# Feature sums of a block-wise feed-forward made tile by tile inside the output projections, one group fewer multiplied plainly, and one block addition moved ahead of the accumulator additions

## The chip, the cores and the metric

One core of a Trainium2 chip runs the whole program. The metric is the device time of one execution in microseconds, the median over runs of the same kernel. A change of 0.2% of it is about 6 us. TensorE multiplies matrices and writes to PSUM; VectorE and ScalarE work on SBUF and PSUM; POOL (GpSimd) works on SBUF; SP only issues transfers.

## The reference, cut to what matters

The model is two blocks over 1024 tokens of width 1024, all in float32. Each block ends with an output projection, a normalised residual, and a feed-forward network. The two networks have the same shape:

```
x = x + _rms_norm(mix, norm_post_mix[i])        # mix = [...] @ w_out
h = _rms_norm(x, norm_pre_ffn[i])
hid = h @ ffn_up                                # 1024 x 1024 times 1024 x 5632
hid = _causal_dwconv(hid, ffn_conv_w, ffn_conv_b)   # 3 taps along the tokens
gate, up = hid[..., :D_FF], hid[..., D_FF:]
f = (gelu(gate) * up) @ ffn_down                # 1024 x 2816 times 2816 x 1024
```

In the second block the activation is a SiLU and only the gate half has the three taps.

## The kernel before

Everything is float32 split into two parts: `hi` is the value rounded by ScalarE to the multiplier's format, `lo` is the rest, and a product is three matmuls: hi times hi, lo times hi, hi times lo.

`project_and_norm` is the output projection. It goes tile by tile over 128 tokens each: 48 matmuls (`product`), then for that tile a residual addition and a normalisation on VectorE with its statistics on ScalarE, then eight transposes on TensorE (`turn`), which put the normalised tile's features in PSUM (`turned`), and a `split` of them: ScalarE writes `hi`, VectorE `lo`. These are the features `blk_hi` and `blk_lo` of the feed-forward. The transposes of a tile stand two products behind its own product.

`feed_forward` handles the 2816 hidden columns in 22 groups of 128. For one group the up-projection has a gate half and an up half, so its weights are a 2 by 2 of blocks (half of the input features by gate and up), and the features are a 2 by 2 of blocks as well (half of the input features by half of the tokens). Groups 0 and 1 (`PLAIN = 2`) are multiplied plainly: two products of 48 matmuls of 512 columns, `plain_product`. All later groups use seven block products of 12 matmuls each in place of eight: P1, P6, P5, P2, P7, P3, P4. Their weight sums (S1 to S4) are made by POOL for each group; the feature sums T1 to T4 are made once. T1 = b12 - b11, T2 = b22 - T1, T4 = b21 - T2 and T3 = b22 - b12, where b11, b12 are the first half of the features for the first and second half of the tokens, and b21, b22 the second half. Before the change `t_sums(c)` makes them by VectorE for one 128-row chunk of features at a time, 10 additions of 128x512 each for four chunks; ScalarE rounds each sum and POOL (for the last chunk VectorE) subtracts.

One group is a `turn` on every engine. On TensorE it is the seven block products with 16 tiles of the down-projection (`down0` to `down15`, three matmuls each, for the group before) in four chunks between them: P1, P6, P5, P2, chunk, P7, chunk, P3, chunk, P4, chunk. VectorE adds each down tile to the accumulator in `x` (`add_down`) and combines the block products: u2 from P6, u3 and c22 from P7, c12 from P3, c21 from P4. The convolution's taps for the first half of the work follow (tapga, tapgb), the product gate times up is `hid`, and its rounding residue `hid_lo`. The first turn (`extra`) does the down-projections of both plain groups, the second one alone at its end. The last three turns ("alone" below) have no down tiles; there `M.skip(pe, j, 4)` stands in for each chunk, and makes TensorE's queue wait until its own last product is complete.

The order on each engine is the order in which the code is written; engines wait for each other on semaphores. `M`, `V`, `A` and `G` count what TensorE, VectorE, ScalarE and POOL have made in a turn. `following.first_dense` and `second_dense` are parts of group 0's first plain product, which are put between the last transposes of the output projection. ffn1 and ffn2, wout1 and wout2 are the names of the two networks and the two output projections.

## Time and profile before

| | us |
|---|---|
| median of 3 runs | 3067.23 (3066.8 to 3067.81) |
| the profiled execution, its own time | 3067.87 |
| its span in the trace | 3066.1 |
| TensorE busy in it | 2939.7 (96%) |
| mean granted TensorE clock | 0.983 |

How to read it: TensorE is the engine to look at. It is busy nearly all the time, and what it waits for in the few places where it does not work is what a change can win back. Busy time counts overlapped matmuls, so what a stretch costs is read from the starts of its rows.

### The profile page before, as it was taken

The numbers are of one execution on the slowest core, as the hardware profiler recorded it, in microseconds if no ns is written. First come the engines' busy times: TensorE is split into PE (matmuls) and PEld (weight loads), VectorE is DVE, ScalarE is ACT, GpSimd is POOL, SyncE is SP. The second block draws the span as 40 slices with busy tenths as digits, with TensorE's granted clock in tenths as the row PEclk, the third lists the DMA queues.
The fourth block names the chain that finished last, engine by engine and source line by source line (L and its number), as shares of the span: only waits on it lengthen the run. The fifth ranks groups of instructions, "written<-read, shape, count | busy, mean of one in ns | idle before, by whom it ended". The sixth has DMA issues, their size and how long they took to land. (4 is left out here: it accounts for less than half of the span.)

```text
span 3066.1 us, 55422 instructions
## 1 busy us (share of the span) xinstructions
PE 2939.7 (96%) x21756; PEld 2529.1 (82%) x21756; DVE 1974.5 (64%) x2682; ACT 1199.4 (39%) x1857; POOL 1198.7 (39%) x1035
## 2 busy tenths in 40 slices
PE   8999999996999999979999999999999799999998
PEld 6787888785788888768999999998978688888876
DVE  6898865567677777656465656663436666666644
ACT  3132544433233333343456555554323232323233
POOL 0003322325465656531343433432122455555562
PEclk9999999998999999999999999999999799999999
DMA  4111000311111112133111110112430111111112
GB/s 130 44 48 29 3 16 12 138 55 38 49 58 44 58 44 58 41 104 105 42 43 49 36 43 29 49 47 78 154 104 28 45 55 48 56 46 58 45 45 83
DMA packets 205489, 173.24 MB, mean 57 GB/s; under 512 B 10589, under 2 KB 182197, under 8 KB 204917
## 3 DMA queue, kind: packets, MB, share of 16 engines
q1 hardware_dynamic: 198389, 162.02, 17.2%
q10 hardware_dynamic: 6912, 8.52, 0.8%
q8 instruction: 142, 2.33, 0.3%
q14 instruction: 46, 0.38, 0.0%
HBM read 149.41 MB, written 21.10 MB: 56 GB/s over the span
## 5 line engine op out<-in xcount | busy, mean ns | idle before, releaser
L2930 DVE TENSOR_TENSOR tokens_x<-ffn_acc,tokens_x 128x512 f32<-128x512 f32 x450 | 296.4, 684 | 112.6 <-PE ffn_acc L2460 112.4
L3759 PE MATMUL mix_e<-blk_hi,mix_w_hi 128*128 128x348 f32 (+3 forms) x1056 | 346.8, 328 | 3.6 <-DVE blk_lo L2854 2.9
L3759 PE MATMUL mix_e<-blk_lo,mix_w_hi 128*128 128x348 f32 (+3 forms) x1056 | 339.8, 322 | 0.0
L3759 PE MATMUL mix_e<-blk_hi,mix_w_lo 128*128 128x348 f32 (+3 forms) x1056 | 338.9, 321 | 0.0
L2443 PE MATMUL ffn_out<-ffn_T,ffn_w12h 128*128 128x512 f32 x960 | 302.4, 396 | 21.5 <-DVE ffn_y L2898 7.5
L2460 PE MATMUL ffn_acc<-blk_hi,ffn_hid_hi 128*128 128x512 f32 x900 | 311.9, 396 | 9.3 <-DVE tokens_x L2930 5.7
L2443 PEld LDWEIGHTS ffn_out<-ffn_T,ffn_w12h 128*128 128x128 f32 x960 | 181.5, 191 | 62.8 <-POOL ffn_w12l L2362 15.6
L2362 POOL TENSOR_TENSOR ffn_w03l<-ffn_r,ffn_w03h 128x512 fp32r<-128x512 f32 x120 | 176.0, 1467 | 127.9 <-ACT ffn_w03h L2677 126.9
L2362 POOL TENSOR_TENSOR ffn_w12l<-ffn_r,ffn_w12h 128x512 fp32r<-128x512 f32 x120 | 174.3, 1462 | 122.5 <-ACT ffn_w12h L2677 110.2
L3285 POOL TENSOR_TENSOR mix_w_lo<-mix_raw,mix_w_hi 128x1024 fp32r<-128x1024 f32 x44 | 107.1, 2434 | 279.6 <-ACT mix_w_hi L3337 279.4
L2460 PEld LDWEIGHTS ffn_acc<-blk_hi,ffn_hid_hi 128*128 128x128 f32 x900 | 170.8, 190 | 46.7 <-issue 6.0
L3759 PEld LDWEIGHTS mix_e<-blk_hi,mix_w_hi 128*128 128x128 f32 x1056 | 199.1, 189 | 8.3 <-DVE blk_lo L2854 3.2
L3759 PEld LDWEIGHTS mix_e<-blk_lo,mix_w_hi 128*128 128x128 f32 x1056 | 199.0, 188 | 0.3
L3759 PEld LDWEIGHTS mix_e<-blk_hi,mix_w_lo 128*128 128x128 f32 x1056 | 198.9, 188 | 0.0
L2443 PE MATMUL ffn_out<-ffn_T,ffn_w12l 128*128 128x512 f32 x480 | 189.8, 396 | 0.0
L2460 PE MATMUL ffn_acc<-blk_hi,ffn_hid_lo 128*128 128x512 f32 x450 | 176.9, 393 | 0.0
L3300 POOL TENSOR_TENSOR mix_work<-mix_sf 128x128 f32<-128x128 f32 (+1 forms) x192 | 84.0, 437 | 209.9 <-DVE mix_sf L3600 181.5
L599 DVE SCALAR_TENSOR_TENSOR mixed_conv<-in_c,top_table,mixed_conv 128x1024 f32<-128x1024 f32 x120 | 155.9, 1299 | 3.8
L2677 ACT ACTIVATE ffn_w12h<-ffn_r 128x512 fp32r<-128x512 f32 x118 | 72.1, 625 | 213.2 <-PE ffn_out L2443 193.2
L2443 PE MATMUL ffn_out<-blk_hi,ffn_w03h 128*128 128x258 f32 (+1 forms) x480 | 130.1, 326 | 10.5 <-POOL ffn_w03l L2362 9.3
L2362 POOL TENSOR_TENSOR ffn_w12l<-ffn_S,ffn_w12h 128x512 fp32r<-128x512 f32 x40 | 53.6, 1341 | 208.3 <-ACT ffn_w12h L2677 194.2
L2677 ACT ACTIVATE ffn_w03h<-ffn_r 128x512 fp32r<-128x512 f32 x116 | 72.9, 630 | 155.1 <-PE ffn_out L2443 95.2
(494 smaller groups left out, 7493.3 us busy)
## 6 DMA issues: line engine op xcount, KB each, us to landing
ffn_r<-ffn_up SPq DMA_DIRECT2D x88, 256.0 KB, 3.0
mix_raw<-w_in SPq DMA_DIRECT2D x44, 512.0 KB, 3.9
ffn_r<-w_up SPq DMA_DIRECT2D x88, 256.0 KB, 3.0
ffn_room<-ffn_down SPq DMA_DIRECT2D x20, 512.0 KB, 4.0
ffn_room<-w_down SPq DMA_DIRECT2D x20, 512.0 KB, 3.9
proj_w_raw<-w_in_first SPq DMA_DIRECT2D x19, 512.0 KB, 3.8
branch_gates<-proj SPq DMA_DIRECT2D x16, 520.0 KB, 4.8
wout_raw<-w_out SPq DMA_DIRECT2D x16, 512.0 KB, 3.7
```

Of the source, the lines that this page charges most:

```text
L599: nc.vector.scalar_tensor_tensor(conv[:, f, :], c[:, f, t:t + T], table[:, column:column + 1], conv[:, f, :], ALU.mult, ALU.add).then_inc( ...
L2362: G.by(tt(slots[slot_][1], raw, slots[slot_][0], ALU.subtract), f"lo_{name}")
L2443: mm = nc.tensor.matmul(o, a[:, k, :], rhs, start=fresh and k == 0 and part == 0, stop=k == half - 1 and part == 2, skip_group_check=True)
L2460: mm = nc.tensor.matmul(accs[t % len(accs)], a[:, par, i * P:(i + 1) * P], b[:, h, :], start=part == 0, stop=part == 2)
L2677: A.by(activation(slots[slot_][0], raw, ACT.Copy), f"hi_{name}")
L2930: return vec.tensor_tensor(dst, accs[t % len(accs)], dst, ALU.add)
L3285: tt(w_lo[n % 2][:], raw[:], w_hi[n % 2][:], ALU.subtract).then_inc(lo_ready, 1)
L3300: tt(d4[:, :, 0, :], ref, a4[:, :, 0, :], ALU.subtract)
L3759: last = nc.tensor.matmul(dst[:, 0:m], a[n % 2][:, kd, :], b[:, kd, c:c + m], start=kd == 0 and part_ == 0, stop=kd == KD - 1 and part_ == 2)
```

## The change

The diff does seven things.

1. The feature sums are made by tiles of 128 tokens (all four feature chunks at once, still 128x512 elements an operation), `token_sums`, from the transposed tile in PSUM rather than from hi and lo in SBUF: T1a = b12(PSUM) - h11, T1 = T1a - l11, T2 = b22(PSUM) - T1, T3a = b22(PSUM) - h12, T3 = T3a - l12, T4a = h21 - T2, T4 = T4a + l21. That is 7 operations for each of 4 tile pairs, 28 in place of 40. Tile 4 pairs with tile 0, 5 with 1, 6 with 2, 7 with 3.
2. The output projections take the tiles in the order 0, 1, 4, 2, 5, 3, 6, 7 (the second one with the 16 meta rows third), and the sums of tiles 4 and 5 stand inside the projection's loop, those of 6 and 7 behind it. The transposes of a tile move from two products behind to inside the next product, before its last chunk.
3. ScalarE rounds T2, T1, T3 of tiles 4 and 5 at the end of the projection (`early_hi`), POOL subtracts them there (`early_lo`); the remaining lo parts of tiles 6 and 7 (8 operations) are VectorE's (`DVE_LO`), T4 of tiles 4 and 5 POOL's.
4. The raw sums lie in places that are free then, some of them those of the weights of group 0's second product. Therefore `second_load` waits for POOL's first two early subtractions, and ScalarE rounds those weights after six.
5. Only group 0 is plain. The first turn does group 1, with the down-projection of group 0; there is no extra down-projection. TensorE waits for each T before the first product that needs it (`wait_block`), and for `plain_tap` (the taps of the plain group) before P1 and P6.
6. In every turn, VectorE's s5 = P5 + x stands ahead of `down0` to `down3`, and c22 = P7 + s5 follows P7; u3 is gone. P3, which adds to P5's bank, waits for s5 rather than for c22, and P4 for c22 rather than u3.
7. In the alone turns TensorE's queue waits for its own completion only once, behind P4 (and not in the last).

```
-    tile_at = [0, 1, NT] + list(range(2, NT)) if meta_src is not None else list(range(NT))
+    tile_at = [0, 1, NT, 4, 2, 5, 3, 6, 7] if meta_src is not None else [0, 1, 4, 2, 5, 3, 6, 7]
...
             for i in range(2, tiles):
                 if mixed or i > 2:
                     pe.wait_ge(psum_free, i - (1 if mixed else 2))
-                for k in order:
+                for n, k in enumerate(order):
+                    if i == 2 and n == KD - 1:
+                        turn(0)
+                    if i == 3 and n == 3:
+                        turn(1)
+                    if i >= 3 and n == KD - 1:
+                        turn(i - 1)
                     mm = product(i, k)
                 mm.then_inc(product_ready, 1)
-                turn(i - 2)
-            turn(tiles - 2)
...
+                before = tile_at[i - 1] if 0 < i < tiles - 1 else None
+                if before in (4, 5):
+                    following.token_sums(dve, before, turned_of(i - 1), ("T1a", "T3a"))
+                if i == tiles - 1:
+                    following.token_sums(dve, 5, turned_of(i), ("T4a", "T4"))
...
+                if before == 4:
+                    following.token_sums(dve, 4, turned_of(i - 1), ("T1", "T2", "T3", "T4a", "T4"))
+                if before == 5:
+                    following.token_sums(dve, 5, turned_of(i - 1), ("T1", "T2", "T3"))
...
+            for name in names:
+                dst, a, b, op, after = ways[name]
+                if after:
+                    dve.wait_ge(t_step, summed(t, after))
+                vec.tensor_tensor(dst, a, b, op).then_inc(t_step, 1)
...
                 def downs(chunk):
                     if not has_down:
-                        M.skip(pe, j, 4)
+                        if chunk == 3 and not last:
+                            M.skip(pe, j, 2 * NT)
                         return
...
                 G.wait(pe, j, "lo_P3")
-                V.wait(pe, j, "c22")
+                V.wait(pe, j, "s5")
                 M.by(block_product(1, b22, [bank_c], False), "P3")
                 downs(2)
                 G.wait(pe, j, "lo_P4")
-                V.wait(pe, j, "u3")
+                V.wait(pe, j, "c22")
...
                 downs(3)
-                if extra:
-                    pe.wait_ge(extra_lo, 1)
-                    pe.wait_ge(plain_hid_lo, 2)
-                    V.wait(pe, j, DOWN[-1])
-                    for t in range(2 * NT):
-                        if t >= len(accs):
-                            pe.wait_ge(extra_added, t - len(accs) + 1)
-                        down_tile(1, t).then_inc(extra_down, 1)
...
+                M.wait(dve, j, "P5")
+                if second and first:
+                    dve.wait_ge(plain_hid_lo, 1)
+                    dve.wait_ge(plain_hid_hi, 1)
+                elif second:
+                    V.wait(dve, j, "hid_lo")
+                V.by(vec.tensor_tensor(uu[:, 512:T], bank_c, xbuf, ALU.add), "s5")
                 downs(0, 1, 2, 3)
                 M.wait(dve, j, "P7")
...
             V.skip(dve, 0, len(dve_names))
-            t_sums(0)
+            for t, name in DVE_LO[0:4]:
+                t_split_lo(dve, vec.tensor_tensor, t, name, t_dve_lo)
             plain_taps(0)
-            t_sums(1)
+            for t, name in DVE_LO[4:]:
+                t_split_lo(dve, vec.tensor_tensor, t, name, t_dve_lo)
             plain_taps(1)
             plain_hidden(0)
             plain_hidden_lo(0)
-            t_sums(2)
-            plain_taps(2)
-            t_sums(3)
```

How VectorE's order moves between the first output projection and the first network. Before, from the last normalisation (L2098) and the last two splits to the plain group's taps (L2898):

```order
L2098 SCALAR_TENSOR_TENSOR wout1_normed_7158<-tokens_x_49,wout1_inv_7161,wout1_gains_7164 128x1024
L2066 TENSOR_TENSOR blk1_lo_51<-wout1_out2,blk1_hi_50 128x8x128
L2066 TENSOR_TENSOR blk1_lo_51<-wout1_turned0,blk1_hi_50 128x8x128
...
L2861 TENSOR_TENSOR ffn1_t_raw0_7150<-blk1_hi_50 128x512
L2861 TENSOR_TENSOR ffn1_t_raw0_7150<-ffn1_t_raw0_7150,blk1_lo_51 128x512 x2
...
L2861 TENSOR_TENSOR ffn1_t_raw3_7153<-ffn1_t_raw3_7153,blk1_lo_51 128x512 x2
L2898 SCALAR_TENSOR_TENSOR ffn1_y_7142<-ffn1_out0,top_table,ffn1_y_7142 128x1023
```

Now, from the last residual addition (L2110) over the last normalisation (L2122) to the same taps (L2956); `ffn1_acc` is the transposed tile in PSUM:

```order
L2110 TENSOR_TENSOR tokens_x_49<-wout1_scaled_7173,tokens_x_49 128x1024
L2459 TENSOR_TENSOR ffn1_t_place1_7151<-blk1_hi_50,ffn1_t_low4_7162 128x512
L2459 TENSOR_TENSOR ffn1_t_place1_7151<-ffn1_t_place1_7151,blk1_lo_51 128x512
...
L2122 SCALAR_TENSOR_TENSOR wout1_normed_7168<-tokens_x_49,wout1_inv_7171,wout1_gains_7174 128x1024
L2459 TENSOR_TENSOR ffn1_t_place2_7152<-ffn1_acc,blk1_hi_50 128x512
...
L2083 TENSOR_TENSOR blk1_lo_51<-ffn1_acc,blk1_hi_50 128x8x128
...
L2428 TENSOR_TENSOR ffn1_T2_7137<-ffn1_y_7142,ffn1_T2_7137 128x4x128
...
L2956 SCALAR_TENSOR_TENSOR ffn1_y_7142<-ffn1_out0,top_table,ffn1_y_7142 128x1023
```

Between the last normalisation and the taps of group 0 there stand now the split of tile 7, 14 sums of tiles 6 and 7 and four lo parts; before it was two splits and ten sums, with thirty more sums behind the taps. Two sums (T4a and T4 of tile 5) stand ahead of the last normalisation.

VectorE in a turn, from u2 to c22. Before:

```order
L2961 TENSOR_TENSOR ffn1_ug_7143<-ffn1_out1,ffn1_room_7149 128x512
L2930 TENSOR_TENSOR tokens_x_49<-ffn1_acc,tokens_x_49 128x512 x4
L2976 TENSOR_TENSOR ffn1_uu_7144<-ffn1_out1,ffn1_room_7149 128x512
L2978 TENSOR_TENSOR ffn1_uu_7144<-ffn1_out0,ffn1_uu_7144 128x512
L2930 TENSOR_TENSOR tokens_x_49<-ffn1_out1,tokens_x_49 128x512
```

Now:

```order
L3019 TENSOR_TENSOR ffn1_ug_7143<-ffn1_out1,ffn1_room_7149 128x512
L3033 TENSOR_TENSOR ffn1_uu_7144<-ffn1_out0,ffn1_room_7149 128x512
L2988 TENSOR_TENSOR tokens_x_49<-ffn1_acc,tokens_x_49 128x512 x4
L3037 TENSOR_TENSOR ffn1_uu_7144<-ffn1_out1,ffn1_uu_7144 128x512
L2988 TENSOR_TENSOR tokens_x_49<-ffn1_out1,tokens_x_49 128x512
```

The first addition into `uu` now reads P5's bank (`out0`) and stands ahead of the four accumulator additions; one addition, not two, follows P7.

TensorE at the end of the first output projection, before: the last product, the transposes of tiles 5 and 6, then group 0's first matmuls.

```order
L1968 MATMUL wout1_out1<-wout1_w_lo3_77,blk1_hi_50 128x512 x2
L1984 MATMUL wout1_turned0<-top_ident,wout1_normed_7158 128x128 x8
L1984 MATMUL wout1_out2<-top_ident,wout1_normed_7158 128x128 x8
L2425 MATMUL ffn1_out0<-blk1_hi_50,ffn1_w03h_7130 128x512
```

Now:

```order
L1971 MATMUL wout1_out1<-wout1_w_lo2_76,blk1_hi_50 128x512 x2
L1990 MATMUL ffn1_acc<-top_ident,wout1_normed_7168 128x128 x8
...
L1971 MATMUL wout1_out1<-wout1_w_lo3_77,blk1_hi_50 128x512 x2
L2530 MATMUL ffn1_out0<-blk1_hi_50,ffn1_w03h_7130 128x512
```

The transposes of tile 6 stand ahead of the last six matmuls of the last product, and none stand between it and group 0. In both kernels tile 7's transposes follow 24 matmuls later.

## Rows read from the trace of the kernel before

**Rows 1.** Busy time by stretch: start:end, length, each engine's busy us, PEclk granted, DMA.

```profile
641.00:652.95 11.95, 11.95 (x57) 9.86 (x56) 5.26 (x6) 3.77 (x7) 0.96 (x1) 1.00 0.11 44
680.60:701.40 20.80, 12.83 (x49) 10.01 (x49) 17.37 (x15) 5.62 (x7) 7.60 (x5) 0.83 0.09 25
811.73:842.00 30.27, 30.27 (x134) 24.81 (x133) 22.67 (x28) 10.66 (x15) 18.20 (x13) 1.00 0.18 53
...
2456.60:2487.10 30.50, 30.50 (x158) 25.98 (x156) 17.54 (x25) 9.78 (x14) 16.64 (x12) 1.00 0.17 52
```

**Rows 2.** Timeline of TensorE, start of ffn1: start, us, line, [idle before <- who ended it].

```profile
652.95 1.03 PE L1984 MATMUL wout_turned<-top_ident,wout_normed 128*128 128x128 f32 x8
680.59 0.80 PE L2425 MATMUL ffn_out<-blk_hi,ffn_w03h 128*128 128x512 f32 x1 [2.44 <-POOL ffn_w03l L2347]
701.39 1.22 PE L2425 MATMUL ffn_out<-blk_hi,ffn_w12h 128*128 128x512 f32 x2 [7.97 <-POOL ffn_w12l L2347]
720.05 0.80 PE L2443 MATMUL ffn_out<-blk_hi,ffn_w03h 128*128 128x512 f32 x1 [4.62 <-POOL ffn_w03l L2362]
732.75 1.19 PE L2443 MATMUL ffn_out<-ffn_T,ffn_w12h 128*128 128x512 f32 x2 [7.54 <-DVE ffn_y L2898]
768.72 0.77 PE L2460 MATMUL ffn_acc<-blk_hi,ffn_hid_hi 128*128 128x512 f32 x1 [5.65 <-DVE tokens_x L2930]
781.47 0.40 PE L2443 MATMUL ffn_out<-blk_hi,ffn_w03h 128*128 128x512 f32 x1
```

**Rows 3.** The same for the start of ffn2.

```profile
2336.39 1.91 PE L1984 MATMUL wout_turned<-top_ident,wout_normed 128*128 128x128 f32 x16
2377.70 1.22 PE L2425 MATMUL ffn_out<-blk_hi,ffn_w12h 128*128 128x512 f32 x2 [4.64 <-POOL ffn_w12l L2347]
2396.36 0.80 PE L2443 MATMUL ffn_out<-blk_hi,ffn_w03h 128*128 128x258 f32 x2 [4.64 <-POOL ffn_w03l L2362]
2408.86 1.19 PE L2443 MATMUL ffn_out<-ffn_T,ffn_w12h 128*128 128x512 f32 x2 [7.50 <-DVEq L2918]
2442.91 0.80 PE L2460 MATMUL ffn_acc<-blk_hi,ffn_hid_hi 128*128 128x512 f32 x1 [3.62 <-POOL blk_hi L2395]
2456.58 0.40 PE L2443 MATMUL ffn_out<-blk_hi,ffn_w03h 128*128 128x258 f32 x2
```

**Rows 4.** VectorE's feature sums in 663 to 742 by form, then timeline rows of VectorE and POOL.

```profile
L2861 DVE TENSOR_TENSOR ffn_t_raw<-ffn_t_raw,blk_lo 128x512 f32<-128x512 f32 x24 | 28.3, 1179 | 0.8
...
668.78 0.69 DVE L2861 TENSOR_TENSOR ffn_t_raw<-ffn_t_raw,blk_lo 128x512 f32<-128x512 f32 x1
669.51 1.67 DVE L2861 TENSOR_TENSOR ffn_t_raw<-blk_hi,ffn_t_raw 128x512 f32<-128x512 f32 x1
676.22 2.60 DVE L2898 SCALAR_TENSOR_TENSOR ffn_y<-ffn_out,top_table,ffn_y 128x1023 f32<-128x1023 f32 x2
...
669.14 3.18 POOL L2355 TENSOR_TENSOR ffn_T<-ffn_t_raw,ffn_T 128x512 fp32r<-128x512 f32 x2 [3.12 <-ACT ffn_T L2635]
676.92 1.30 POOL L2355 TENSOR_TENSOR ffn_T<-ffn_t_raw,ffn_T 128x512 fp32r<-128x512 f32 x1 [2.02 <-ACT ffn_T L2635]
```

**Rows 5.** Timeline of VectorE: the normalisation of the last tile, wout1 and wout2.

```profile
659.11 1.28 DVE L2098 SCALAR_TENSOR_TENSOR wout_normed<-tokens_x,wout_inv,wout_gains 128x1024 f32<-128x1024 f32 x1
...
2340.08 1.28 DVE L2098 SCALAR_TENSOR_TENSOR wout_normed<-tokens_x,wout_inv,wout_gains 128x1024 f32<-128x1024 f32 x1
```

**Rows 6.** Timeline of TensorE in the first alone turns of ffn1, and c21 on VectorE.

```profile
1265.63 0.40 PE L2443 MATMUL ffn_out<-blk_hi,ffn_w03h 128*128 128x512 f32 x1
1277.16 0.70 PE L2443 MATMUL ffn_out<-ffn_T,ffn_w03h 128*128 128x512 f32 x2 [0.30 <-PEq L118]
1281.78 0.47 PE L2443 MATMUL ffn_out<-blk_hi,ffn_w12h 128*128 128x512 f32 x1 [1.60 <-DVEq L118]
1292.22 0.70 PE L2443 MATMUL ffn_out<-ffn_T,ffn_w12h 128*128 128x512 f32 x2 [0.84 <-DVEq L118]
...
1291.39 0.69 DVE L2990 TENSOR_TENSOR ffn_uu<-ffn_out,ffn_room 128x512 f32<-128x512 f32 x1
```

More of the change, by code:

```diff
@@ L2267, in sync, with turn @@
         def sync(sp):
-            def turn(g, par, has_down, extra=False, last=False):
+            def turn(g, par, has_down, first=False, last=False):
                 j = turn_of(g)
-                if extra:
-                    sp.wait_ge(t_step, 10 * half)
-                    sp.wait_ge(plain_up, 2 * PLAIN)
+                if first:
+                    sp.wait_ge(plain_up, 2)
                     load_down(sp, 0)
@@ L2376, in next_group, with turn @@
                 G.by(tt(R12, R12, R11, ALU.subtract), "S4")
-            def turn(g, par, has_down, extra=False, last=False):
+            def turn(g, par, has_down, first=False, last=False):
                 j = turn_of(g)
@@ L2462, in down_tile, with turn @@
                 return mm
-            def turn(g, par, has_down, extra=False, last=False):
+            def turn(g, par, has_down, first=False, last=False):
                 j = turn_of(g)
@@ L2490, in turn @@
                 V.wait(pe, j, "c21", back=1)
-                if extra:
-                    pe.wait_ge(t_lo_ready, 4 * half)
-                    pe.wait_ge(plain_tap, 2 * PLAIN)
+                if first:
+                    wait_block(pe, "T2")
+                    pe.wait_ge(plain_tap, 2)
                 M.by(block_product(1, block_t(T2_), [bank_b], True), "P6")
@@ L2671, in last_split, with turn @@
                     last_hi_ready, 1)
-            def turn(g, par, has_down, extra=False, last=False):
+            def turn(g, par, has_down, first=False, last=False):
                 j = turn_of(g)
@@ L2930, in add_down, with turn @@
                 return vec.tensor_tensor(dst, accs[t % len(accs)], dst, ALU.add)
-            def turn(g, par, has_down, extra=False, last=False):
+            def turn(g, par, has_down, first=False, last=False):
                 j = turn_of(g)
```

309 lines of the change are left out of this document (165 added, 144 removed), and 3 rows, old and new, of the table SUM_STEPS.

## Prediction

> **What bounds the kernel now.** I read the windows first. In a turn of either network TensorE is busy for all of its 30.27 us (ffn1, 132 matmuls: 0.229 each) or 30.50 us (ffn2), at the full clock, 2.4 GHz, while VectorE has 22.67 and less [rows 1]. The loop's turns are at TensorE's own pace, so whatever is only hidden work there is worth nothing. A projection tile is the same: TensorE busy 11.95 of 11.95 us, VectorE 5.26 [rows 1]. TensorE's timeline then shows where it does wait, and that is in one place per network: between the end of the output projection and the first turn of the loop. In ffn1 the last projection product ends at 652.95 and the turn of group 3 starts at 781.47: 128.5 us, with five waits of 2.44, 7.97, 4.62, 7.54 and 5.65, together 28.2 us [rows 2]. In ffn2 it is 2336.39 to 2456.58, 120.2 us, with 4.64, 4.64, 7.50 and 3.62, 20.4 us [rows 3]. The waits cost more than themselves: after the first, 48 matmuls take from 680.59 until 7.97 before 701.39, so 12.8 us, where 48 times 0.229 is 11.0 [rows 2]; the granted clock of this stretch is 0.83, a part of it at 1.2 GHz after an engine that stood still [rows 1].
>
> How much of it is loss: three sets of transposes 2.4 us (1.91 for two of them, [rows 3]), four plain products at 11.0 (44.0; group 0's first, in pieces, about 0.3 more), a turn 30.3 and 48 down matmuls 11.0, sum 88.0. So 40 us of ffn1's 128.5 are waits and slow clock. For ffn2 the same count, a little more for its gate products of 72 shorter matmuls, gives 89.5 of 120.2, so 31 us.
>
> The waits name POOL's weight residues and `plain_tap`, and both are late for the same reason. VectorE is busy 17.37 of 20.80 us in such a stretch [rows 1], with sums; they are also slower than they need be. A sum takes 0.69 us, but 1.67 when POOL subtracts at the same time; the 24 of one form have a mean of 1.179 [rows 4]. The tap operations, two in 2.60, are not slowed though POOL runs inside them at 676.92: they read one operand from PSUM, the sums two from SBUF [rows 4]. By the Trainium skill (SBUF — State Buffer, Who interferes with whom) a VectorE instruction with two SBUF inputs and a POOL instruction that reads SBUF exclude each other for a whole instruction, one with at most one SBUF input does not; the trace agrees, with 0.98 us more for a sum and nothing for a tap. I count 0.95 for each such meeting.
>
> **The parts.** Times are from P, the end of the last projection product. In the new kernel two transposes that followed it come before it, so P itself is 1.6 us later (two times 0.8); it is added at the end.
>
> *Sums of tiles 4 and 5 in the projection.* 14 operations of 0.72 (0.69 and a gap) in tiles where VectorE idles 6.7 of 11.95 us [rows 1]: hidden, except that the transposes of the tile after tile 4 overwrite its PSUM and wait for its T2. That is ready at about P+7.4 of that tile plus two to three operations, 9 to 10 us; the transposes come at 7/8 of the next product, 9.6. I take 0.5 us per projection, 1 together; if all of it is exposed, 2.
>
> *The last tile.* Before, its normalisation ends at 660.39, 7.4 us after P [rows 2, 5], just what two sets of transposes and 24 matmuls (1.9 + 5.5) cover. Now only 5.5 cover it, so TensorE waits 1.9 in any case. T4a and T4 of tile 5 and POOL's six early subtractions (1.30 each, [rows 4]) now fall there as well; three two-SBUF operations that meet POOL give 3 us more. So the transposes at P+10.5 in ffn1. In ffn2, which has no first normalisation, it ended at 2341.36, P+5.0 [rows 3, 5]; ScalarE's rounding of the tile before no longer stands in this chain (half a microsecond), two meetings give 1.9: P+6.4. The slow clock after such a wait costs 1.8, as at 680.59 (12.8 for 11.0); I count 1.9.
>
> *VectorE from there to P6.* In ffn1: 14 sums and 8 lo parts of 0.72 (15.8), the split 1.2, two pairs of taps 5.2: 22.2. Sixteen of these operations read two SBUF operands. POOL has less to do than before, but its group sums S1 to S4 and weight residues fall here: I take six meetings (5.7), between none and 16 (15.2). P6 waits for the second taps: 10.5 + 22.2 + 5.7 = 38.4. TensorE's own work until P6 is 10.5 + 0.8 + 5.8 + 11.0 + 2.7 + 1.9 = 32.7, so it waits 5.7 around P1. In ffn2 one pair of taps (2.6) and a multiplication (1.4): 6.4 + 15.8 + 1.2 + 2.6 + 1.4 + 5.7 = 33.1.
>
> *The rest, to the loop's same point* (the start of the turn of group 3). After P6's start 30.3 less P1's 2.8, the turn of group 2, and the slow clock: 48 matmuls took 720.05 - 4.62 - 701.39 = 14.0 after the wait of 7.97 and 781.47 - 768.72 = 12.8 after that of 5.65, where 11.0 is the full clock's, so 3.0 and 1.8 [rows 2]; I take 2.3 and 2.0. ffn1: 38.4 + 27.5 + 30.3 + 2.3 + 1.6 = 100.1, against 128.5: **28.4 won**. ffn2: 33.1 + 27.6 + 30.5 + 2.0 + 1.6 = 94.8 against 120.2: **25.4 won**. Of each, 2.7 us are matmuls that no longer exist (12 of 0.229); the rest is waits and clock. The weights of group 0's second product, now loaded later, need six POOL subtractions (until P+11 to 13), a rounding and a POOL subtraction of twice the size (2 x 1.30, [rows 4]): ready about P+16, while the first product ends at 10.5 + 0.8 + 5.8 + 1.9 = P+19. Hidden by 3 us in ffn1, some 1 to 2 in ffn2; without that cover they would cost what they exceed it by.
>
> *s5 ahead of the down additions.* In the loop P3 begins one chunk of 12 matmuls (2.7 us) after P7 ends, and u3 and c22 take 1.4: hidden already, worth nothing. VectorE waits for `down0` there, so s5 costs nothing either. In the alone turns no chunk covers it: P7 to P3 takes 1281.78 - 1277.16 = 4.6, of which 2.7 are matmuls and 1.6 the wait [rows 6]. But P6 of the next turn starts when c21 is done (1291.39 + 0.69 = 1292.08, P6 at 1292.22, [rows 6]), and c21 stands behind taps whose inputs come from POOL's and ScalarE's chain that starts at P7's end. So in the first two alone turns the gap moves from P3 to P6, and only the last turn keeps 1.6 to 2. The queue's wait ahead of P7 (1265.63 to 1277.16 is 11.5 for 48 matmuls, 11.0) is won three times: 0.5 each. Together 3.5 per network, 7 for both; if no chain takes P3's place 3 x 2.5 x 2 = 15, if the end of the network is also bound elsewhere, 2.
>
> **The sum.** 28.4 + 25.4 + 7 - 1 = 59.8; from the profiled execution's own time, 3067.9, that is 3008.1. The median of the runs shown is 0.6 lower, so **3007.5**.
>
> Bounds of the likeliest case: one to two meetings more or less in each network and the alone turns at 2 or 15 give about 2996 to 3018.
>
> **The rivals.** *VectorE is not the bound* (15%). For it: the sums from PSUM do not meet POOL, and there are only 14 left. Then TensorE's own work sets P6, 27.7 at P+7.4 without a slow clock, VectorE's 29.6; P6 at 29.6 and no clock loss is 8.8 + 2.3 better in ffn1, and in ffn2 the same count gives 27.4 in place of 33.1 and 2 of clock, 7.7: 3007.5 - 18.8, about 2989. Against it: VectorE was the busiest engine here.
>
> *Every two-SBUF operation meets POOL* (17%): ten more meetings a network, 9.5 each, 19: 3026. The Trainium skill's page SBUF — State Buffer (SBUF: two separate sides) says that whichever of the two starts first keeps the port for its whole instruction; the 0.98 us above agree. For it: a mean of 1.179 against 0.69 is half of those sums met already [rows 4]. Against: the eight lo parts start before P1's weights are free for POOL.
>
> *The early sums stretch the projections* (5%): if every tile from the fourth on waited 1 to 2 us for its transposes, ten tiles, 3018 to 3028. The windows' 6.7 idle us of VectorE speak against it.
>
> *Slower* (4%): s5 must be done before P3, and stands ahead of four accumulator additions, on which `down5` to `down8` wait. If in the loop VectorE came to it late, all 32 looped turns would stretch; it decides from 59.8 / 32 = 1.9 us a turn on. With 2.5 us each, 80 in all, it would be 3088. Against it: VectorE idles 7.6 us of a turn [rows 1], and P5 ends one whole product before the chunk whose additions it precedes.
>
> *The change does little* (2%): if the waits at the start stay where they are because the last taps alone set them, only the removed matmuls and the alone turns count, 12 us: 3055; and no change within 0.2% at all would need these to be lost too.
>
> **How the numbers follow.** Likeliest case 57%. Range 2990 to 3026: from the first rival to the second; outside it remain half of the first rival, a part of the second, and the last three. A measurement tells 6 us, 0.2%, from no change. Faster 0.95, same 0.01, slower 0.04.
>
> **What would show it.** Right: the span from P to the turn of group 3 near 100 and 95 us, TensorE's waits there three (before tile 7's transposes, before P1, before P6), VectorE without idle from P to the taps, a loop turn of 30.3 and 30.5 as before, a P7 to P3 of 2.7 in the alone turns with a longer wait before P6. Wrong: TensorE waiting inside the projections, a POOL weight residue as the last releaser, or a turn in the loop longer than 30.5.

## The result, and the profile after

The changed kernel takes 3022.88 us (median of 4 runs, 3017.51 to 3025.36); the kernel before, timed beside it, takes 3067.02. The ratio is 0.985 (0.9838 to 0.9862), 44 us less. Timed once more beside other kernels it took 3018.50 (5 runs, 3013.22 to 3019.09) against 3066.84: 0.9838 (0.9822 to 0.9853), 48 us less. The prediction was 3007.5, with 59.8 us won.

P is again the end of the last projection product. The windows of the changed kernel (start:end, length, busy time of PE, PEld, DVE, ACT, POOL, granted clock, DMA), for the stretches of [rows 1]: a projection tile, the stretch from tile 7's transposes to P6, a looped turn of ffn1 and one of ffn2:

```profile
649.60:661.55 11.95, 11.95 (x57) 9.83 (x56) 5.34 (x7) 3.88 (x7) 0.95 (x1) 1.00 0.11 44
671.80:701.60 29.80, 24.20 (x116) 20.84 (x117) 29.31 (x29) 14.13 (x20) 21.02 (x14) 0.84 0.09 26
790.86:821.13 30.27, 30.27 (x134) 24.80 (x132) 23.15 (x29) 10.95 (x15) 18.46 (x13) 1.00 0.19 53
2442.62:2473.12 30.50, 30.50 (x157) 26.00 (x156) 20.62 (x26) 9.79 (x14) 17.39 (x13) 1.00 0.17 53
```

Tile and turns last as long as before. VectorE is busy 29.31 of 29.80 us before P6, so it is what TensorE waits for there. TensorE's timeline at the start of ffn1, to set beside [rows 2] (P; tile 7's transposes; P1 and P6 of the first turn; the turns of groups 2 and 3):

```profile
661.55 0.40 PE L2530 MATMUL ffn_out<-blk_hi,ffn_w03h 128*128 128x512 f32 x1
671.82 1.97 PE L1990 MATMUL ffn_acc<-top_ident,wout_normed 128*128 128x128 f32 x8 [4.50 <-DVE wout_normed L2122]
696.37 0.77 PE L2548 MATMUL ffn_out<-blk_hi,ffn_w03h 128*128 128x512 f32 x1 [5.58 <-DVE ffn_y L2956]
701.63 0.76 PE L2548 MATMUL ffn_out<-ffn_T,ffn_w12h 128*128 128x512 f32 x2
729.28 0.40 PE L2548 MATMUL ffn_out<-blk_hi,ffn_w03h 128*128 128x512 f32 x1
...
760.59 0.40 PE L2548 MATMUL ffn_out<-blk_hi,ffn_w03h 128*128 128x512 f32 x1
```

Five long waits have become two, and P to the turn of group 3 is 99.04 us, where it was 128.5. The same view of ffn2, to set beside [rows 3]; here it is 95.15 us for 120.2:

```profile
2316.96 0.32 PE L2530 MATMUL ffn_out<-blk_hi,ffn_w03h 128*128 128x344 f32 x1
2323.77 1.97 PE L1990 MATMUL wout_turned<-top_ident,wout_normed 128*128 128x128 f32 x8 [2.81 <-DVE wout_normed L2122]
2348.55 0.77 PE L2548 MATMUL ffn_out<-blk_hi,ffn_w03h 128*128 128x258 f32 x2 [3.72 <-DVE ffn_y L2953]
...
2412.11 0.40 PE L2548 MATMUL ffn_out<-blk_hi,ffn_w03h 128*128 128x258 f32 x2
```

Timeline rows of VectorE, then of POOL, in the same stretch of ffn1, for [rows 4, 5]: the first sum ahead of the last normalisation, that normalisation, a lo part, the second taps; and POOL's early subtractions:

```profile
666.10 1.78 DVE L2459 TENSOR_TENSOR ffn_t_place<-blk_hi,ffn_t_low 128x512 f32<-128x512 f32 x1
669.67 2.10 DVE L2122 SCALAR_TENSOR_TENSOR wout_normed<-tokens_x,wout_inv,wout_gains 128x1024 f32<-128x1024 f32 x1
690.28 1.76 DVE L2428 TENSOR_TENSOR ffn_T<-ffn_y,ffn_T 128x512 fp32r<-128x512 f32 x1
698.54 2.59 DVE L2956 SCALAR_TENSOR_TENSOR ffn_y<-ffn_out,top_table,ffn_y 128x1023 f32<-128x1023 f32 x2
...
663.79 3.54 POOL L2428 TENSOR_TENSOR ffn_T<-ffn_t_low,ffn_T 128x512 fp32r<-128x512 f32 x2 [5.69 <-ACT ffn_T L2424]
668.97 5.15 POOL L2428 TENSOR_TENSOR ffn_T<-ffn_t_low,ffn_T 128x512 fp32r<-128x512 f32 x3
```

Operations of VectorE with two SBUF operands take 1.76 and 1.78 here where a sum alone took 0.69 [rows 4], and the normalisation 2.10 for 1.28 [rows 5]; the taps are not slowed. POOL's subtractions take 1.7 each in place of 1.30: a meeting (such an operation of VectorE at the same time as one of POOL) costs both engines. TensorE and, in the last row, c21 on VectorE in the first turns of ffn1 without down tiles, for [rows 6]:

```profile
1264.55 0.47 PE L2548 MATMUL ffn_out<-blk_hi,ffn_w03h 128*128 128x512 f32 x1 [0.30 <-PEq L118]
1271.37 0.70 PE L2548 MATMUL ffn_out<-ffn_T,ffn_w12h 128*128 128x512 f32 x2 [3.79 <-DVEq L118]
1291.17 0.51 PE L2548 MATMUL ffn_out<-blk_hi,ffn_w03h 128*128 128x512 f32 x1 [1.45 <-POOL ffn_w03l L2470]
1298.59 0.69 PE L2548 MATMUL ffn_out<-ffn_T,ffn_w12h 128*128 128x512 f32 x2 [4.37 <-DVEq L118]
...
1270.53 0.69 DVE L3049 TENSOR_TENSOR ffn_uu<-ffn_out,ffn_room 128x512 f32<-128x512 f32 x1
```

No row waits at P3 any more; P6 waits 3.79 and 4.37, until c21 is done (1271.22). Cutting the three profiled executions (before; after; after once more, the run e7 below) at the same points gives, with turn 19 the first one without down tiles, and the "last transposes" those of the first full tile of tokens at the end of ffn1:

| stretch | before | after | after, e7 |
|---|---|---|---|
| start of the program to P | 652.95 | 661.55 | 654.68 |
| P to the turn of group 3, ffn1 | 128.52 | 99.04 | 95.89 |
| the loop, to turn 19 | 484.16 | 484.18 | 484.20 |
| turn 19 to the last transposes of ffn1 | 105.99 | 106.61 | 105.89 |
| from there over the second mixer to P | 964.77 | 965.58 | 965.32 |
| P to the turn of group 3, ffn2 | 120.19 | 95.15 | 95.37 |
| the loop, to turn 19 | 488.32 | 488.32 | 488.32 |
| turn 19 to the end | 121.20 | 121.87 | 121.73 |
| span | 3066.1 | 3022.3 | 3011.4 |

All that is won is won in the two starts. Beside it P of ffn1 comes 1.7 us later (652.95 to 654.68 in e7) and P of ffn2 0.6 to 0.8 (964.77 to 965.32 and 965.58), for the transposes that now stand ahead of it. Two things stand against the prediction: the turns without down tiles gave nothing, and the first execution lost 7 us before P in code that the change leaves alone.

### The profile page after: what moved, and what is told of

It reads as the page before. It is cut to its first block and busy times, and to the rows that moved or that the text cites. A ratio compares the mean times of both kernels' runs of the same rounds, so it can differ in the third digit from the quotient of the medians.

```text
span 3022.3 us, 55409 instructions
## 1 busy us (share of the span) xinstructions
PE 2926.2 (97%) x21732; PEld 2524.8 (84%) x21732; DVE 1964.6 (65%) x2675; ACT 1204.0 (40%) x1872; POOL 1215.0 (40%) x1045
## 5 line engine op out<-in xcount | busy, mean ns | idle before, releaser
L2548 PE MATMUL ffn_out<-ffn_T,ffn_w12h 128*128 128x512 f32 x1008 | 316.6, 396 | 13.4 <-DVEq L118 13.4
L2470 POOL TENSOR_TENSOR ffn_w03l<-ffn_r,ffn_w03h 128x512 fp32r<-128x512 f32 x126 | 186.3, 1479 | 138.0 <-ACT ffn_w03h L2776 129.9
L2548 PEld LDWEIGHTS ffn_out<-ffn_T,ffn_w12h 128*128 128x128 f32 x1008 | 191.3, 191 | 54.5 <-issue 14.6
L2470 POOL TENSOR_TENSOR ffn_w12l<-ffn_r,ffn_w12h 128x512 fp32r<-128x512 f32 x126 | 183.1, 1464 | 126.7 <-ACT ffn_w12h L2776 117.4
L2548 PE MATMUL ffn_out<-ffn_T,ffn_w12l 128*128 128x512 f32 x504 | 199.4, 396 | 0.0
L2548 PE MATMUL ffn_out<-blk_hi,ffn_w03h 128*128 128x258 f32 (+1 forms) x504 | 136.6, 326 | 11.7 <-DVE ffn_y L2956 5.6
```

The costliest lines, as they stand in the source:

```text
L2470: G.by(tt(slots[slot_][1], raw, slots[slot_][0], ALU.subtract), f"lo_{name}")
L2548: mm = nc.tensor.matmul(o, a[:, k, :], rhs, start=fresh and k == 0 and part == 0, stop=k == half - 1 and part == 2, skip_group_check=True)
```

## The experiments

Each kernel was timed beside the kernel before, in three groups that each ran on one chip. Medians: first group, before 3066.68, e1 to e4; second, before 3066.84, e5 to e8; third, before 3068.78, e9 to e11. Lengths in the texts are those of the one profiled execution of each kernel.

How far such lengths differ by themselves is to be seen where the code is that of the changed kernel. P to the turn of group 3 took 99.04 and 95.89 in its own two executions, and 97.18, 97.64 and 96.92 in e3, e5 and e8, for ffn1; for ffn2 95.15, 95.37, 96.84, 95.46 and 95.91. Turn 19 to the last transposes of ffn1 took 106.61 and 105.89, and 107.21, 105.51, 106.06 and 105.18 in e4, e6, e9 and e10; turn 19 to the end in ffn2 121.87 and 121.73, and 123.32, 121.84, 120.35 and 121.77. A single length inside these ranges tells nothing of an edit.

**e1: s5 alone, in the kernel before.**

```
                 G.wait(pe, j, "lo_P3")
-                V.wait(pe, j, "c22")
+                V.wait(pe, j, "s5")
...
                 G.wait(pe, j, "lo_P4")
-                V.wait(pe, j, "u3")
+                V.wait(pe, j, "c22")
...
+                V.by(vec.tensor_tensor(uu[:, 512:T], bank_c, xbuf, ALU.add), "s5")
                 downs(0, 1, 2, 3)
                 M.wait(dve, j, "P7")
-                V.by(vec.tensor_tensor(uu[:, 512:T], bank_b, xbuf, ALU.add), "u3")
...
```

> The kernel before with the one edit that s5 (P5 + x) stands ahead of down0 to down3, P3 waits for s5, P4 for c22, and u3 is gone. Theory A (in the turns without down tiles the end is set by the chain P7, weight sums, convolution, taps, c21, so a wait taken from P3 comes back at P6): the wait of 1.6 before P3 is gone there, the one before P6 of the next turn grows from 0.8 to 3 or 4 us, and the time stays at that of the kernel before, 3067 within 3. Rival B (the edit does win in these turns, and the loss of the first part of the program hid it): 2 to 3.5 us in each network, 3060 to 3063. In the loop both expect turns of 30.27 and 30.50.

3066.89, ratio 1.000 (0.9991 to 1.0009). In ffn1 the wait before P6 grew from 0.84 to 2.13 in turn 20 and from 3.81 to 4.37 in turn 21, and P1 of turn 21 waited 1.94. A looped turn is 30.26 and 30.52. In ffn2 turn 19 to the end took 119.81 for 121.20, the only gain in it; in ffn1 turn 19 to the last transposes took 107.98 for 105.99, so what ffn2 won ffn1 lost. Theory A holds for the time and the place (its 3 to 4 us before P6 were too many, a part of it stands before P1); B's 2 to 3.5 us a network did not come.

**e2: the changed kernel without s5** (the same edit backwards).

> The changed kernel without the s5 edit: u3 and c22 behind P7 again, all else as changed. Theory A: nothing lost, 3023 within 3; the wait before P3 in the turns without down tiles is back at 1.6 and that before P6 falls from 3.8 and 4.4 to about 1 to 2. Rival B: 4 to 7 us lost, 3027 to 3030.

3016.74, ratio 0.9833 (0.982 to 0.9847). Nothing is lost without it (the 3023 of the expectation was the changed kernel's first median; its second one is 3018.5, see e7). The waits before P6 in ffn1 are 1.63 and 4.35, so only the first shrank; turn 19 to the last transposes is 106.3, as with it.

**e3: c21 ahead of the taps in the turns without down tiles.**

```
+                if not has_down:
+                    M.wait(dve, j, "P4")
+                    V.by(vec.tensor_tensor(uu[:, 0:512], bank_b, xbuf, ALU.add), "c21")
                 downs(8)
                 A.wait(dve, j, "convg")
                 tap(y0, ug, 0, 1, "tapga")
...
```

> The changed kernel, with c21 ahead of both gate taps on VectorE in the three turns of each network that have no down tiles; nothing is left out. Theory A (c21 stands in the queue behind the taps and so holds P6): the waits of 3.8 and 4.4 before P6 in ffn1, 2.7 and 2.6 in ffn2, go. What of it is won at the end depends on the next chain: in ffn1 hid, its rounding and POOL's residue for P3 are done only 2 to 2.5 us before the P3 of now, so about 1 us a turn; in ffn2 no second pair of taps stands ahead of hid, so most of the 2.7. Together 5 to 8 us, 3015 to 3018. Rival C (all of the waits are won): 13 us, 3010. Rival D (the end of each network is set by the load of the last weights alone): 3023 within 2.

3016.77, ratio 0.9841 (0.9827 to 0.9854). TensorE's waits in turns 20 and 21 of ffn1 of this kernel: P6, P5, then P1 of turn 21:

```profile
1259.26 0.73 PE L2556 MATMUL ffn_out<-ffn_T,ffn_w12h 128*128 128x512 f32 x2 [0.28 <-POOL ffn_w12l L2478]
1264.73 0.73 PE L2556 MATMUL ffn_out<-ffn_T,ffn_w12h 128*128 128x512 f32 x2 [2.45 <-POOLq L119]
1282.07 0.80 PE L2556 MATMUL ffn_out<-blk_hi,ffn_w03h 128*128 128x512 f32 x1 [3.12 <-POOL ffn_w03l L2478]
```

P6's wait is gone, as A said, but P5 now waits 2.45 and P1 3.12 for weight residues of POOL, and turn 19 to the last transposes is 106.60, against 106.61. In ffn2 no wait before P6 is left either, P5 waits 2.58 and 2.37 in its place, and the end comes 122.53 after turn 19, where e7 has 121.73. My 5 to 8 us were wrong; the nearest is D, though what sets the end is more than the load (e8).

**e4: only T2's lo parts ahead of the taps.**

```
-            for t, name in DVE_LO[0:4]:
+            for t, name in DVE_LO[0:2]:
                 t_split_lo(dve, vec.tensor_tensor, t, name, t_dve_lo)
             plain_taps(0)
-            for t, name in DVE_LO[4:]:
-                t_split_lo(dve, vec.tensor_tensor, t, name, t_dve_lo)
             plain_taps(1)
+            for t, name in DVE_LO[2:]:
+                t_split_lo(dve, vec.tensor_tensor, t, name, t_dve_lo)
...
```

> The changed kernel with another order on VectorE between the feature sums and the first turn: only the two lo parts of T2 stand ahead of the plain group's taps, the other six behind both pairs; ScalarE does the second convolution before the activation. Nothing is left out. Theory E (VectorE's queue sets P1 and P6): in ffn1 the second taps end about 5 us earlier, so P6 of the first turn starts at 34 to 36 after the last projection product in place of 40.1, and the wait of 5.6 before P1 falls to 2; in ffn2 the wait of 3.7 before P1 falls below 1. With less slow clock behind the waits 8 to 12 us won, 3011 to 3015. Rival F (POOL's residue of P1's or P6's weights is ready no earlier): at most 3 us, 3020 or more.

3018.24, ratio 0.9841 (0.9828 to 0.9855). P6 of the first turn, in ffn1 and in ffn2:

```profile
690.33 1.22 PE L2548 MATMUL ffn_out<-ffn_T,ffn_w12h 128*128 128x512 f32 x2 [2.92 <-POOL ffn_w12l L2470]
...
2344.43 1.19 PE L2548 MATMUL ffn_out<-ffn_T,ffn_w12h 128*128 128x512 f32 x2 [5.46 <-DVEq L2977]
```

In ffn1 P6 is at P+35.9 as expected (P is 654.46) and P1 does not wait, yet the turn of group 3 comes at 96.59, no earlier than in e7 (95.89): P6 now waits for POOL, and it and P5 run at a granted clock of 0.79, 7.2 us for 24 matmuls. In ffn2 I had overlooked that P6 waits for the product gate times up (L2977), which the edit put behind six lo parts; the turn of group 3 comes at 96.67 there, 1.3 later than in e7. 8 to 12 us were expected, nothing measurable came.

**e5: TensorE waits for itself at each chunk**, as before the change.

```
-                        if chunk == 3 and not last:
-                            M.skip(pe, j, 2 * NT)
+                        M.skip(pe, j, 4)
...
```

> The changed kernel, but in the turns without down tiles TensorE's queue waits for its own completion at each of the four chunks, as it did before the change. Theory A (the chain through ScalarE, VectorE and POOL sets the end of each network): not measurable, within 2 us of the changed kernel timed beside it. Rival: the 0.5 us for each wait count, 6 such waits in each network, up to 6 us lost.

3016.80, ratio 0.9835 (0.982 to 0.985). No loss; turn 19 to the end of ffn2 is even 119.87, as in e1, where the changed kernel has 121.73. The windows show why. First e7, P6 to P2 of turns 20 and 21 of ffn2, behind a wait of 2.73 and 2.41; then the same of e5, behind 1.07 and 0.99:

```profile
2915.45:2922.63 7.18, 7.17 (x24) 5.72 (x25) 3.15 (x3) 3.33 (x6) 4.09 (x3) 0.76 0.13 39
2939.76:2946.94 7.18, 7.18 (x24) 5.76 (x25) 3.14 (x3) 3.32 (x6) 4.08 (x3) 0.76 0.01 2
```

```profile
2919.13:2924.71 5.58, 5.58 (x24) 4.51 (x25) 3.14 (x3) 3.33 (x6) 4.13 (x3) 1.00 0.03 8
2942.05:2947.64 5.59, 5.59 (x24) 4.51 (x25) 3.14 (x3) 3.33 (x6) 4.13 (x3) 1.00 0.01 3
```

With 0.3 us waited at each chunk, less was left to wait before P6, and the same 24 matmuls took 5.58 us at the full clock, not 7.18 at 0.76. The change had gathered small waits into one, behind which a part ran at 1.2 GHz. In ffn1 the same edit gave nothing: 1.96 and 3.27 were left to wait before P6, both were followed by 0.76, and turn 19 to the last transposes is 106.18.

All profiled executions together bear this out, with one exception. Before P6 of turns 20 and 21, ten waits of 0.8 to 1.6 us were followed by a clock of 1.00 and at most 6.0 us for the 24 matmuls; 32 of 33 waits of 2.4 us and more by 0.63 to 0.79 and 6.9 to 8.4 us. The 33rd, 2.64 in e9, was followed by the full clock, and around 2 us both occur (1.96 slow, 2.06 in e11 and 2.13 in e1 not). So of the 1.9 us that e5 is ahead of e7, e9 had 1.4 without the edit.

**e6: POOL's early subtractions behind the last normalisation.**

```
                     if i == NT - 1:
+                        pool.wait_ge(normed_ready, tiles)
                         following.early_lo(pool)
...
```

> The changed kernel, with POOL's six early subtractions behind the normalisation of the last tile, not beside it; nothing is left out. Theory G (what the meetings of POOL and VectorE cost is real, but they can only be moved): the last tile's transposes start at 7.4 to 8 after the last projection product in ffn1 in place of 10.3, and the three operations ahead of them take 0.7, 0.7 and 1.3 in place of 1.8, 1.6 and 2.1; then group 0's second product waits for its weights, which need the six subtractions, about 5 us, and the turn of group 3 comes no earlier than now, up to 3 us later in each network. In time 0 to 6 us more than the changed kernel beside it. Rival H (the normalisation is the whole of the loss): 3 us earlier in each network, 6 us less.

3015.01, ratio 0.983 (0.9815 to 0.9845). The last normalisation and then group 0's second product in ffn1 (P is 655.18):

```profile
662.68 1.09 PE L1992 MATMUL ffn_acc<-top_ident,wout_normed 128*128 128x128 f32 x8 [1.76 <-DVE wout_normed L2124]
675.68 1.22 PE L2532 MATMUL ffn_out<-blk_hi,ffn_w12h 128*128 128x512 f32 x2 [6.22 <-POOL ffn_w12l L2399]
```

The two sums and the normalisation took 0.68, 0.69 and 1.28, the transposes came at P+7.5 in place of 10.3, and the second product waited 6.22 for its weights. The turn of group 3 came at 97.14 (e7: 95.89), in ffn2 at 95.51 (95.37). Theory G: nothing is won by moving the meetings. The median is 3.5 us below the changed kernel's beside it, which their intervals do not tell apart.

**e7: the changed kernel again.**

> The changed kernel itself, nothing edited, timed beside the others. Theory J (the 6.7 us that its first profiled execution lost before the output projection, in a part that the change leaves alone, belong to that execution): its trace has the first output projection at 564 to 565, as the kernel before, and the median is 3016 to 3019. Rival (they belong to the program, by where its code or buffers lie): the output projection at 570 again, and 3021 to 3024.

3018.50, ratio 0.9838. The start to P is 654.68, as the table shows, so the first part's loss belongs to an execution and not to the program. Windows of 180 to 240 and 300 to 360 us, in the first profiled execution and in e7, the same code in both:

```profile
180.00:240.00 60.00, 59.09 (x261) 48.23 (x260) 54.98 (x48) 16.50 (x19) 0.00 (x0) 0.94 0.16 45
300.00:360.00 60.00, 56.01 (x1235) 50.52 (x1231) 48.68 (x62) 33.25 (x56) 25.92 (x16) 0.94 0.01 3
```

```profile
180.00:240.00 60.00, 59.09 (x275) 48.44 (x274) 54.37 (x49) 17.04 (x21) 0.00 (x0) 1.00 0.17 45
300.00:360.00 60.00, 57.47 (x1386) 52.70 (x1382) 50.43 (x68) 30.73 (x50) 23.23 (x16) 1.00 0.01 3
```

TensorE is as busy, but was granted 0.94 of the clock and got through fewer matmuls. (The kernel before was granted 0.97 and 1.00 in these two stretches.) The profiled execution of e10 has the same 0.94 in both and its first output projection at 570.32, as the first one of the changed kernel (570.74); in the eleven other profiled executions, that of before and e1 among them, it is at 563.6 to 565.0. That it was a matter of the execution is shown; what made the clock differ is not. That the median of 3018 to 3019 is right for the changed kernel and 3022.88 a little high is likely, as all variants with a similar stretch lie at 3015 to 3018.5.

**e8: ScalarE's order at the end of each network.** The roundings for P3 and P4 of the last turn stand ahead of that of hid, and the last down weights ahead of the last hid:

```
+            last_split(3)
             act.wait_ge(last_hid, 1)
             activation(hid20[1][:, 0, :], staged, ACT.Copy).then_inc(last_hid_hi, 1)
-            last_split(3)
...
```

> The changed kernel with another order on ScalarE at the end of each network: in the last turn the roundings for P3 and P4 stand ahead of that of hid (so that POOL frees the buffers of the last down weights earlier), and the rounding of the last down weights stands ahead of that of the last hid. Nothing is left out. Theory K (the end of each network hangs on the chain of hid, POOL's last residues, the load of the down weights and its rounding): the wait of 4.1 for POOL's last residue in ffn1 falls below 2, 2 to 3 us won in ffn1 and 0.5 to 1 in ffn2. Rival (hid alone sets the end): nothing.

3015.83, ratio 0.9835 (0.9817 to 0.9852). The transposes of the meta rows at the end of ffn1, the place where POOL's last residue was waited for, in e7 and then in e8:

```profile
1324.06 1.03 PE L2651 MATMUL ffn_out<-top_ident,ffn_meta 16*128 16x16 f32 x8 [4.05 <-POOL ffn_T L2515]
```

```profile
1324.11 1.00 PE L2659 MATMUL ffn_out<-top_ident,ffn_meta 16*128 16x16 f32 x8 [4.26 <-DVE ffn_meta L2949]
```

POOL is no longer the releaser, but the rows' normalisation on VectorE is, with as long a wait (4.26). Turn 19 to the last transposes is 104.59 for 105.89, 0.6 below the lowest of the executions without this edit; in ffn2 nothing (121.97). K had said 2 to 3 and 0.5 to 1, so about half of it in ffn1 and none in ffn2.

**e9: T4a and T4 of tile 5 behind the last normalisation.**

```
-                if i == tiles - 1:
-                    following.token_sums(dve, 5, turned_of(i), ("T4a", "T4"))
                 inverse(i, 2 * i, std_ready, inv_ready)
...
+                if i == tiles - 1:
+                    following.token_sums(dve, 5, turned_of(i), ("T4a", "T4"))
...
                 act.wait_ge(t_pool_lo, 6)
+                act.wait_ge(t_step, summed(5, "T4"))
```

> The changed kernel, with T4a and T4 of tile 5 behind the normalisation of the last tile on VectorE, not ahead of it; the rounding of group 0's second weights waits for them. Nothing is left out. Theory L (VectorE's sum of work sets P6, the transposes do not): tile 7's transposes start near 8.3 after the last projection product in place of 10.3, P6 of the first turn still at 37 to 39, and the turn of group 3 at 95 to 97: no change in time beyond 2 us. Rival (the transposes set what follows): 2 us earlier in each network.

3015.94, ratio 0.9828 (0.9813 to 0.9843). The transposes at P+8.15 as expected; P6 at P+39.6 and the turn of group 3 at 98.41 in ffn1, within what the start of ffn1 takes without the edit, but 34.5 and 94.07 in ffn2, 1.3 earlier than in e7 and 1.1 below the lowest. In ffn1 theory L holds in so far as nothing was won, in ffn2 some of it was won; the sum is not measurable.

**e10: e4's order, with ffn2's product gate times up ahead of the last four lo parts.**

> As the kernel with the taps first, but in ffn2 the product gate times up also stands ahead of the last four lo parts (there it is what releases P6: with the taps first it came 5.5 us too late). Theory E: in ffn2 P6 at 34 to 35 after the last projection product in place of 36.8, and the turn of group 3 at 93 to 94.5 in place of 95.4; ffn1 as with the taps first, P6 at 35.9 but the turn of group 3 near 96.5, since the wait only moves. About 1 to 2 us in all, below what the timing tells. Rival M (each earlier wait comes back as slow clock): 95.4 again in ffn2.

3016.05, ratio 0.9822 (0.9808 to 0.9837), although its profiled execution had the low clock in the first part. P6 of the first turn in ffn2 (P is 2312.48):

```profile
2344.29 0.70 PE L2548 MATMUL ffn_out<-ffn_T,ffn_w12h 128*128 128x512 f32 x2 [0.47 <-DVEq L2977]
```

It is at P+31.81 in place of 36.83 (34 to 35 were expected), and the turn of group 3 at 92.63, 2.7 us earlier than in e7; in ffn1 97.79, where e4 had 96.59. So VectorE's order does set P6 in ffn2; half of the 5 us reach the loop.

**e11: all together** (e10, e9, e8 and e5).

> All edits that looked useful together, in the changed kernel: taps first with ffn2's product ahead, T4a and T4 of tile 5 behind the last normalisation, ScalarE's order at the end of each network, and TensorE's wait for itself at each chunk of the turns without down tiles (which kept the clock at full speed there). Expected from the single ones: 1.5 us at the end of ffn1, 1.5 to 2 in ffn2's last turns, 1 to 2 at the starts, so 4 to 6 us below the changed kernel's 3018.5, 3012 to 3015. If they all end in the same next chain: 3016 to 3018.

3010.50 (5 runs, 3008.18 to 3011.33), ratio 0.9807 (0.9793 to 0.9821). It is faster than the changed kernel's 0.9838: all its runs are below all runs of the variants beside it (3013.59 at the least), and below those of the other groups (3012.15, in e8). It is 1.5 us below what was expected. By stretches, against e7: ffn1's start 95.14 for 95.89, ffn2's 93.20 for 95.37, turn 19 to the end 119.85 for 121.73, end of ffn1 105.61 for 105.89. The starts and ffn2's end are below every execution without these edits; e8's gain at the end of ffn1 is not seen again. It is the best version: 5 us below the changed kernel by the profiled executions, 8 by the medians (3018.50, another group).

## Why the prediction was right or wrong

*Right in kind: the two starts.* The step "P to the turn of group 3" was put at 98.5 and 93.2 without the shift of P; measured are 99.04 and 95.89 in ffn1, 95.15 and 95.37 in ffn2. Of the 59.8 us, 53.8 were to come from here, less 1 in the projections; the table gives 29.5 + 25.0 in the first execution and 32.6 + 24.8 in e7. The shift of P is to be taken from that, 1.7 in ffn1 and 0.8 or 0.6 in ffn2, where 1.6 was predicted for each: 52 and 55. The projections have no wait inside, VectorE 5.34 us of 11.95: the 1 us set aside for them was not spent, and the rival of stretched projections fell.

*The last tile.* Transposes were predicted at P+10.5 and P+6.4; they came at P+10.27 and P+6.81. Three two-SBUF operations meet POOL there in ffn1, as said. e6 and e9 show that this place does not set what follows in ffn1: the transposes came 2.8 and 2.1 us earlier in them, the turn of group 3 not (97.14 and 98.41, inside the 95.89 to 99.04 without the edits).

*VectorE to P6: the sum came out, its parts did not.* P6 was put at P+38.4 and 33.1; the first execution has 40.08 and 36.87, e7 37.72 and 36.83. I had priced six meetings of 0.95, 5.7 us, over 22.2 us of other work. In ffn1 VectorE needed 29.4 us from the end of the last normalisation to that of the second taps, in e7 27.4, so 7.2 and 5.2 above the 22.2. But by their own rows ten of the sixteen two-SBUF operations were lengthened in the first execution and eight in e7, by 9.2 and 7.2 us in all, and nine in ffn2, by 9.5. What offset it is that operations that meet nothing follow each other in 0.60, not 0.72, so the other work took 20.1. Two errors that nearly cancel, which is luck. The same sum (a T4a), in the first execution and in e7:

```profile
683.46 1.79 DVE L2459 TENSOR_TENSOR ffn_t_place<-blk_hi,ffn_y 128x512 f32<-128x512 f32 x1
```

```profile
676.60 0.68 DVE L2459 TENSOR_TENSOR ffn_t_place<-blk_hi,ffn_y 128x512 f32<-128x512 f32 x1
```

It and the sum behind it make most of the difference between the two executions: 1.79 and 1.66 in the one, 0.68 and 0.69 in the other. The rival "every two-SBUF operation meets POOL" (3026) fell: neither its count of sixteen nor its 9.5 us more in each start came. That the first median, 3022.88, lies near its 3026 has other causes, told below. "VectorE is not the bound" fell too. The Trainium skill (SBUF — State Buffer, Who interferes with whom) says that the issue order decides which side blocks. The trace agrees in so far as each side is the slowed one in turn: POOL's subtractions went from 1.30 to 1.7, which I had not counted.

*The slow clock stood elsewhere.* I had three waits in ffn1, two are seen in the first execution; in e7 P1 waits 2.37 and P6 0.36. Behind the wait before P1, P1 ran at a granted clock of 0.50 (1.2 GHz). The windows of P1 in ffn1 and in ffn2:

```profile
696.37:701.63 5.26, 5.26 (x13) 4.07 (x13) 5.11 (x7) 3.19 (x4) 2.52 (x2) 0.50 0.02 6
2348.55:2353.83 5.28, 5.28 (x25) 5.28 (x25) 4.16 (x7) 3.15 (x4) 3.09 (x2) 0.50 0.11 31
```

That is 5.26 us in place of 2.75, and 5.28 in place of 3.0. In ffn1 it was nearly free, since the taps ended at 701.13 and P1 at 701.6. In ffn2 VectorE had released P6 at P+35.0, 1.9 later than predicted (0.4 of it the transposes, the rest the meetings less the faster pace), and the slow P1 put another 1.8 on it. Behind P6 the clock was full: from P6 to the turn of group 3 it took 58.96 and 58.28, where I had 60.1 in both. So in ffn1 an error of +1.7 and one of -1.1 nearly cancel, in ffn2 +3.8 and -1.8 leave 2.0. e10 took the last four lo parts from ahead of ffn2's P6, and two of T1 from ahead of its P1; P1 then waited 0.32 and ran at the full clock, and P6 came 5.0 us earlier.

*s5 in the loop* was right: turns of 30.27 and 30.50, and e1 and e2 show no effect; the rival on the other side fell.

*The step that failed is "alone turns", 3.5 us per network, 7 together, with the bounds 2 to 15.* Measured: +0.6 and +0.7 us in the first execution, -0.1 and +0.5 in e7, so nothing. I had said that the gap moves from P3 to P6 in the first two of them, and it did. The failure is in what I kept beside it. Of the "1.6 to 2 of the last turn" nearly nothing arrived. In ffn1 convg follows c12 on ScalarE, behind a rounding of down weights that waits for their load; after, then before:

```profile
1314.95 1.06 ACT L2769 ACTIVATE ffn_T<-ffn_r 128x1024 fp32r<-128x1024 f32 x1 [5.66 <-DMA ffn_r<-ffn_down]
1315.92 1.23 ACT L2827 ACTIVATE ffn_y<-ffn_ug,top_table 128x1024 f32<-128x1024 f32 x1
```

```profile
1335.08 1.06 ACT L2670 ACTIVATE ffn_T<-ffn_r 128x1024 fp32r<-128x1024 f32 x1 [5.48 <-DMA ffn_r<-ffn_down]
1337.61 1.24 ACT L2730 ACTIVATE ffn_y<-ffn_ug,top_table 128x1024 f32<-128x1024 f32 x1 [1.47 <-DVE ffn_ug L2981]
```

The wait for c12 (1.47) is gone, so convg starts 1.6 us nearer to the rounding. But then the first pair of taps, whose operands all lie in SBUF in a turn, runs beside POOL's residue of these weights and takes 3.81 us for 2.71. The transposes of the meta rows come 0.8 nearer, and the 12 matmuls behind them take 5.06 us for 4.34 at a lower clock (0.53 for 0.63). So from the rounding to the last transposes it is 36.4 us after and 36.5 before. The load itself is issued when POOL has made P4's residue, behind the hid of the turn before; the rounding stands 70.2 us behind turn 19 after and 69.5 before, so up to it nothing was won either.

In ffn2 no wait stood before P6 in these turns. Turn 19 became 2.9 us shorter (22.88 to 19.95), and then waits of 2.73 and 2.56 before P6 and 1.7 us of slow clock behind each took it back: from turn 19 to the first matmul of the last down-projections it is 68.57 us where it was 68.70. So the "0.5 times 3 of queue waits" were worth nothing or less: in a stretch that another chain bounds, a wait taken out of TensorE's queue came back in the next one, and the longer wait mostly lowered the clock (e5). e3 and e8 show that there is no single chain behind it: c21 taken away, POOL's residues of P5 and P1 hold as much; the last residue taken away, VectorE's normalisation. What would win there stays open beyond the 1.3 us of e8 and the 1.9 of e5.

*The rest, some 6 us,* is the difference between the profiled executions and the medians. Between the profiled ones of before and of e7 it is 54.7, between the medians of the same group 48.3: e7's profiled execution (3013.22) was the fastest of its five. I had made the sum against an execution and taken 0.6 for the step to the median. The first part of the program differs by 6 us between executions of the same code, with its granted clock. It was seen in two of thirteen profiled executions; how often it happens in the runs that were not profiled, and whether the new code has it more often than the old, stays open.

Not isolated by a run is how the 57 us of the starts divide between the early sums and the plain group that is gone. That both were needed for the order on VectorE that the trace shows is argued, not shown.

## What to carry to other kernels

Where the profile says that an engine in a stretch is bound by another engine's queue, add up that queue's work to the operation that releases, meetings with POOL included: that gave 99 and 95 us for two starts within 3. Give a removed wait no value in a stretch that a chain through several engines bounds, unless you can name the operation that ends the chain and show that it moves too; here most waits that were taken away came back at the next releaser, and only four small edits together gave a difference that the timing tells, 5 to 8 us. And compare medians with medians: one profiled execution may differ by 6 us in code that nobody changed.
